# A decoder layer's MLP with seven half-size products in place of eight, its rows passed through DRAM

## The reference

```
h = x + rms_norm(m, n_mix_post)
f = square(relu(rms_norm(h, n_ffn_pre) @ w_up)) @ w_down
return h + rms_norm(f, n_ffn_post), new_buf, S_new
```

## Time and profile before

| | |
|---|---|
| runs | 1697.92, 1699.09, 1698.83 us, median 1698.83 |
| profiled execution, span | 1695.9 us (its own time is one of those above, 2 to 3 us more than its span) |
| TensorE matmuls busy | 1634.7 us, 96% of the span, 10272 matmuls recorded |
| VectorE, ScalarE, GpSimd busy | 749.9, 320.5, 678.8 us |
| granted clock of TensorE, mean | 0.989 of full |
| DMA | 101.18 MB, 60 GB/s over the span |

### The profile page before, as it was taken

One profiled execution on the slowest core, in us unless ns is written; L12 is line 12 of the kernel. 1 busy time (PEld: TensorE's weight loads), 2 busy tenths in 40 slices (PEclk: granted clock), 3 DMA queues, 4 the chain that ended last, 5 costly groups with the idle time before them and its releaser, 6 DMA issues.

```text
span 1695.9 us, 26474 instructions
## 1 busy us (share of the span) xinstructions
PE 1634.7 (96%) x10272; PEld 1609.6 (95%) x10272; DVE 749.9 (44%) x907; ACT 320.5 (19%) x407; POOL 678.8 (40%) x548
## 2 busy tenths in 40 slices
PE   5999999999999998999998999999999999999994
PEld 4999999899999997999998999999999999999993
DVE  5898969354482334101515623232232323222338
ACT  4100000422311223000214311011111111110122
POOL 3334444232254223434474334343444434343444
PEclk9999999999999999999999999999999999999997
DMA  4211121123221331111321011111111111111112
GB/s 167 88 50 44 49 57 46 30 76 99 75 94 50 95 105 32 43 49 43 145 75 31 26 51 44 49 43 49 44 45 48 44 49 43 49 43 49 44 26 100
DMA packets 57771, 101.18 MB, mean 60 GB/s; under 512 B 6128, under 2 KB 21232, under 8 KB 57344
## 3 DMA queue, kind: packets, MB, share of 16 engines
q1 hardware_dynamic: 43792, 76.97, 15.6%
q10 hardware_dynamic: 13936, 23.60, 4.2%
HBM read 91.00 MB, written 9.55 MB: 59 GB/s over the span
## 4 chain that ended last, share of the span: by engine, by line
PE 94%; DVE 4%; DMA 1%; issue 1%; ACT 1%; ACTq 0%; SPq 0%; DVEq 0%
PE ps L465 84%; PE ps L723 3%; DVE mix L1549 1%; PE ps L813 1%; PE ps L646 1%; PE ps L565 1%; DVE xn_l L1216 1%; PE ps L564 1%; PE ps L491 1%; PE ps L568 1%; PE ps L579 1%; DMA x_in<-xT_dram 1%; PE ps L549 0%; PE ps L554 0%; DVE x_in L1212 0%
## 5 line engine op out<-in xcount | busy, mean ns | idle before, releaser
L368 POOL TENSOR_TENSOR w_h<-raw,zero 128x512 fp32r<-128x512 f32 x250 | 268.7, 1075 | 928.4 <-PE ps L465 806.4
L371 POOL TENSOR_TENSOR w_l<-raw,w_h 128x512 fp32r<-128x512 f32 x250 | 332.3, 1329 | 19.6
L1504 DVE TENSOR_TENSOR mix<-ps,mix 128x1032 f32<-128x1032 f32 x120 | 147.9, 1233 | 300.6 <-PE ps L465 300.6
L465 PE MATMUL ps<-xn_h,w_h 128*128 128x344 f32 x1128 | 248.2, 326 | 5.0 <-DVE xn_l L1216 4.0
L465 PE MATMUL ps<-xn_l,w_h 128*128 128x344 f32 x1128 | 241.9, 320 | 0.0
L465 PE MATMUL ps<-xn_h,w_l 128*128 128x344 f32 x1128 | 241.0, 320 | 0.0
L465 PEld LDWEIGHTS ps<-xn_h,w_h 128*128 128x128 f32 x1128 | 190.2, 188 | 9.4 <-issue 4.8
L465 PEld LDWEIGHTS ps<-xn_l,w_h 128*128 128x128 f32 x1128 | 191.2, 189 | 0.1
L465 PEld LDWEIGHTS ps<-xn_h,w_l 128*128 128x128 f32 x1128 | 188.8, 188 | 0.0
L465 PE MATMUL ps<-fx_h,w_h 128*128 128x344 f32 x768 | 169.7, 322 | 5.8 <-ACT fx_h L1099 5.4
L465 PE MATMUL ps<-fx_l,w_h 128*128 128x344 f32 x768 | 168.8, 321 | 0.0
(11 more groups left out here) (201 smaller groups left out, 1934.3 us busy)
## 6 DMA issues: line engine op xcount, KB each, us to landing
raw<-wseq_dram SPq DMA_DIRECT2D x264, 256.0 KB, 2.6
rope<-rope_dram ACTq DMA_DIRECT2D x2, 2064.0 KB, 8.1
h_res<-xT_dram ACTq DMA_DIRECT2D x1, 4128.0 KB, 12.8
s_dec<-s_in_dram ACTq DMA_DIRECT2D x16, 256.0 KB, 2.8
v_bc<-v_sample_scratch ACTq DMA_DIRECT2D x16, 256.0 KB, 3.8
rets_dram<-s_dec ACTq DMA_DIRECT2D x16, 256.0 KB, 2.2
x_in<-xT_dram SPq DMA_DIRECT2D x2, 1376.0 KB, 12.9
yT_dram<-h_res SPq DMA_DIRECT2D x3, 860.0 KB, 3.9
```

Source lines behind the costliest of these rows:

```text
L368: pool.tensor_tensor(hi, raw[:, s, :], zero[:, 0:1].broadcast_to([P, SLOT]), ALU.add).then_inc(w_hi, 1)
L371: pool.tensor_tensor(lo, raw[:, s, :], hi.bitcast(F32), ALU.subtract).then_inc(w_split, 1)
L465: out = pe.matmul(pch(g, c), w[a][:, place_, sub * P:(sub + 1) * P], xs[b][:, k, c * CH:(c + 1) * CH], start=(first and n == 0), stop=(las ...
L1504: dve.tensor_tensor(t3(mix[:, m, :]), pset(g), t3(mix[:, m, :]), ALU.add).then_inc(ps_free[g % 2], 1)
```

## The change

The two matrix products of the MLP are each done with Strassen's scheme (in the Winograd form) one level deep: the weights and the rows are cut in halves of channels (4 tiles of 8) and halves of tokens (2 x 516), and seven products of half-size operands replace eight, with sums of quadrants ahead of and behind them.

- Tokens are now cut into halves of 516 and matmuls of 258 tokens (`HT`, `HC`).
- A unit is a pair of output tiles: seven products of 4 k-tiles x 3 parts x 2 matmuls, 168 matmuls of 258 columns. The first two units of up (`DIRECT`) stay as before, in 344-column matmuls; then there are 14 units of up and 16 of down (`NV` = 30).
- All of up comes first. The hidden rows of each unit are kept as 7 operands, summed on VectorE (`hidden_sums`, 4 sums of 128x516), stored by the SP queue to `uscr` in DRAM (`store_unit`, 264 + 528 + 1056 KB) and loaded back for down, one group of 4 units at a time (`load_operand`, 28 loads of 1032 KB). `h` goes to DRAM and comes back as well (`hscr`), since the down result `fac` takes its place.
- The operands of down are split again: high part on ScalarE (`staged_hi`, 128x4x516), low part on VectorE (`staged_lo`, two of 128x2x516).
- Weight sums are made on VectorE (`first_sums`, `last_sum`, 4 of 128x512 a unit). The high part of a weight slot is now copied by ScalarE (`high`), GpSimd makes the low part alone (`low`), 7 a unit, in a ring of three.
- PSUM is used as three pairs of banks that rotate (`BANKS`); ScalarE and VectorE take the products out (`up_unit`, `down_unit`).
- The final norm goes by two halves of tokens, both after nearly all of down, with fac and h for 516 tokens at a time.

The core of the diff:

```diff
+HT = T // 2
+HC = HT // 2
+QK = KT // 2
+RING = 3
+DIRECT = 2
+UNITS = FFN // P // 2
+UPV = UNITS - DIRECT
+NV = UPV + UNITS
+STEPS = 7
...
+            def store_unit(u):
+                g, j = divmod(u, QK)
+                sp.wait_ge(t_u, 4 * u + 4)
+                sp.dma_start(uscr[g, 0, :, j, :], hq_row(u, 0)).then_inc(st_u[u % 2], 16)
...
+            def product(v, i, between=None):
+                q = STEPS * v + i
+                a, b, c = BANKS[v]
+                n = (a, b, c, a, c, a, a)[i]
+                x, kh, th = X_OF[i]
+                pe.wait_ge(q_lo, q + 1)
...
+                for s in range(2):
+                    if s == 0 or i == 6:
+                        bank_ready(v, i, s)
+                    for kk in range(QK):
+                        for m, (wa, xb) in enumerate(PARTS):
+                            at_ = th * HT + s * HC
+                            out = pe.matmul(ps[:, 2 * n + s, 0:HC], RINGS[q % RING][wa][:, kk * P:(kk + 1) * P],
+                                            OPS[x][xb][:, QK * kh + kk, at_:at_ + HC],
...
+            def low(v, i):
+                q = STEPS * v + i
+                src = (raw[:, 0, :], raw[:, 1, :], sum_y[:], raw[:, 2, :], raw[:, 3, :], sum_x[:], sum_y[:])[i]
+                hi, lo = RINGS[q % RING]
+                pool.wait_ge(q_hi, q + 1)
+                pool.tensor_tensor(lo, src, hi.bitcast(F32), ALU.subtract).then_inc(q_lo, 1)
...
+            def high(v, i):
+                q = STEPS * v + i
+                if q < RING:
+                    act.wait_ge(mm, E_FFN + 1 + q)
+                else:
+                    act.wait_ge(pm, 2 * (q - RING) + 2)
...
+                act.activation(RINGS[q % RING][0], src, ACT.Copy).then_inc(q_hi, 1)
...
+            high(0, 0)
+            high(0, 1)
+            stored(act, 0)
+            direct_out(1, 0, E_FFN + 2)
+            direct_out(1, 1, E_FFN + 4)
+            high(0, 2)
...
+            def first_sums(v):
+                if v:
+                    dve.wait_ge(q_lo, STEPS * v)
+                else:
+                    dve.wait_ge(mm, E_FFN + 4)
...
+            def down_unit(v):
...
+                evicted(dve, v, "e4")
+                add(m2, 0, c, step_done(v, 4))
+                if p == 3 and g + 1 < GROUPS:
+                    staged_lo(STEPS * (g + 1) + 2)
+                evicted(dve, v, "e3")
+                for s in range(2):
+                    dve.wait_ge(pm, step_done(v, 5) - 1 + s)
+                    f = two(fac[:, m2, HALVES[1]])[:, s, :]
+                    dve.tensor_tensor(f, ps[:, 2 * a + s, 0:HC], f, ALU.add).then_inc(ev_d, 1)
...
+            for v in range(UPV):
+                if v == 0:
+                    first_sums(0)
+                    hidden_sums(0)
+                up_unit(v)
+            for v in range(UPV, NV):
+                down_unit(v)
+            root_argument(0, 3)
+            out_norm(0, 3)
+            root_argument(1, BANKS[NV - 1][1])
             out_residual(0)
+            out_norm(1, BANKS[NV - 1][1])
             out_residual(1)
```

More of the change, by code:

```diff
@@ L340, in _ @@
                                  ).then_inc(raw_ld[s], 16)
[L341 to L348, removed]
+            sp.wait_ge(h_dve, CHUNKS)
+            sp.wait_ge(h_pool, CHUNKS)
@@ L731, in _, with up_mms @@
             FX = (fx_h, fx_l)
-            HID = (hid_h, hid_l)
+            def up_mms(c, g, k, slot, first, last):
+                for n, (a, b) in enumerate(PARTS):
+                    out = pe.matmul(pch(g, c), DIRECT_W[slot][a][:, (k % SLOT_TILES) * P:(k % SLOT_TILES + 1) * P],
+                                    FX[b][:, k, c * CH:(c + 1) * CH],
+                                    start=(first and n == 0), stop=(last and n == 2))
+                return out
             for c, j in ((0, 0), (1, 0), (0, 1), (1, 1), (2, 0), (2, 1)):
@@ L748, in _ @@
                     mix_stat(2)
[L750 to L758, removed]
-                        out = tile_mms((slot + m // 2) % HL, FB * (m % 2) + k, HID, FB * (b % 2) + k,
-                                       g + m, k == 0, k == FB - 1)
-                    out.then_inc(mm, 1)
@@ L819, in _ @@
-            out_stat(CHUNKS - 1)
+            for j in range(2):
+                g = G_FFN + 2 + j
+                free_set(pe, g)
+                for half in range(2):
+                    pe.wait_ge(w_split, S_FFN + 4 + 2 * j + half + 1)
+                    for k in range(QK * half, QK * half + QK):
+                        for c in range(CHUNKS):
+                            out = up_mms(c, g, k, 2 * j + half, k == 0, k == KT - 1)
+                    out.then_inc(mm, 1)
+            OPS = ((fx_h, fx_l), (tx_h, tx_l))
@@ new lines, in h_stat, with f_ones @@
+            def h_stat(t):
+                if t == 0:
+                    pe.wait_ge(hs_ad, 2 * KT)
+                else:
+                    pe.wait_ge(h_cp, 1)
+                for s in range(2):
+                    out = pe.matmul(ps[:, 6 + s, 0:HC], ones[:], hms[:, t * HT + s * HC:t * HT + (s + 1) * HC],
+                                    start=True, stop=True)
+                out.then_inc(h_st, 1)
+            def f_ones(row, first, last, n):
+                for s in range(2):
+                    out = pe.matmul(ps[:, 2 * n + s, 0:HC], ones[:], hq_g[:, row, s * HC:(s + 1) * HC],
+                                    start=first, stop=last)
+                return out
@@ new lines, in f_stat_first @@
+            def f_stat_first():
+                pe.wait_ge(f_ad, 6)
+                pe.wait_ge(h_cp, 2)
+                f_ones(0, True, True, 3).then_inc(f_st, 1)
+            for v in range(NV):
+                for i in range(STEPS):
+                    product(v, i, f_stat_first if (v, i) == (NV - 1, STEPS - 1) else None)
+                    if v == 3 and i in (0, 3):
+                        h_stat(i // 3)
+            pe.wait_ge(f_ad, 8)
+            evicted(pe, NV - 1, "e2")
+            f_ones(4, True, False, BANKS[NV - 1][1])
```

812 lines of the change are left out of this document (563 added, 249 removed).

## The result

The changed kernel takes **1687.03 us** (four runs, 1685.12 to 1688.15) beside 1698.38 for the kernel before on the same chip: ratio 0.9938, 95% interval 0.9925 to 0.9951, 11.4 us faster. The forecast was 1658.1, 40.7 us faster. The direction holds and the time lies inside the range, but nearly three quarters of the forecast gain are missing. One execution of an experiment (`e11_gpsimd`) took 3955.7 us, for no reason that is known, and is left out of its numbers.

What follows compares the result with a forecast made beforehand. The MLP was taken as bound by matmul count and start-to-start time, its end by the norm. 977.4 + 13.5 + 1.6 + 615.4 + 1.8 + 16 + 29.5 = 1655.2 us span; median 2.9 above, 1658.1; range 1606 to 1702.

Steps and rivals of the forecast that it cites:

- The price: Time per 258-column matmul at full clock: 122.1 ns taken, 5040 of them 615.4 us; case of 118 to 125 ns, 60%.
- shared supply: Rival on the matmul time: weight load and stream share one supply, 129.1 ns at 258 columns, 1693 us; 15%.
- load that takes 157.9 ns: Rival: the weight load under a stream sets the pace at 157.9 ns whatever the width, 180 us more, 1838; 9%.
- the floor: Rival: the weight load alone sets the lowest time of a matmul, 112 ns, giving 1607 us; 8%.
- The plain unit: In a plain up unit, ScalarE, VectorE, GpSimd and DMA work fits under 20.5 us of matmuls, costed at nothing.
- the ring rival: Rival: the ring of three weight slots waits in every unit, 2.5 us each, 75 us more, 1733; 8%.
- The handover: Between direct units and first product, TensorE idles while unit 0's data is made and stored and relu follows: 13.5 us.
- The seams: Three joins of down groups at 3.3 us each, 10, and up to down, 6: together 16 us, bounds 0 and 40.
- The statistics: 8 f32 statistics matmuls of 258 columns among the fast units, 217 ns each: 1.8 us.
- The direct units: First two units of up in 344-column matmuls at 157.9 ns, ending at 977.4 us.
- The tail: After the last product: last taking, final norm to +24 us, then 1290 KB out in 5.1; 29.5 us.

Runs made afterwards that it cites:

- e11_gpsimd: Changed kernel with GpSimd's low parts of the weights in units 17 and 18 cut to 8 of 512 columns: 1679.28 us, ratio 0.9903.
- e10_first: Changed kernel with unit 0's hidden rows summed before first weight sums and four low parts, copy of h issued behind first fast unit's store: 1669.58 us, 0.9843.
- e12_all: Changed kernel with the edits to joins, first unit, statistics and up-to-down loads together, last up unit's rows made and stored a unit later: 1642.32 us, 0.9684.
- e3_stat: Changed kernel with the column sums of h and their two roots moved from the fourth fast unit to the fifth: 1683.60 us, 0.9918.

## Why the prediction was right and wrong

- **The price.** Right in kind, too dear. 122.1 was chosen over 118.4; measured 119.8, between the two: of the surplus over 2.4 GHz, 3.7 ns go with the matmul by the line above and the rest with the columns. It gave back 11.6 us. The rivals on the price are settled: no shared supply (it gives 129.1 ns at 258 columns, and by its formula 214 at 512 where 232.0 were measured), no load that takes 157.9 ns; the floor exists, but at 258 columns the stream is just above it.
- **The plain unit** costed at nothing: right. Units 4 to 12 have no idle time in 181 us, so the ring rival is false.
- **The handover**, 13.5 against 13.0: right by its size, for a reason that was half wrong. I had the data made in 5.2 us and the store land 6.7 us later, on a free queue. They took 4.6 and 7.2, so two errors cancel (the profile counts the store as 1806 KB, not 1848). The sum left out the copy of h issued ahead of the store, so it gave no hint that making the data earlier would not help.
- **"The seams. [...] Together 16; bounds 0 and 40"** is the step that failed: 47.1 us were measured, 17.9 from up to down and 29.2 at the three joins, outside the bounds. It is the whole of what is missing: the span is 30.3 us over the forecast, and the seams are 31.1 over it. I compared a single third low part with one product (4.7 against 2.93), as if VectorE were on time when it began; the two before it had already used the slack, and VectorE began the taking ahead of it 1.8 us after TensorE had finished the product. In the next unit I summed the operations that exclude each other (21.9 against 20.5) but set VectorE's takings, 4.9 us, at nothing; the unit takes 24.0. I counted neither the half clock behind each break nor, from up to down, that ScalarE's taking stands behind the operand it waits for.
- **The statistics**, 1.8: only the matmuls were costed, as 8 of 217 ns, where the trace has 8 in unit 3 and 4 in unit 29: each f32 matmul of the program stands there as two (the 24 in the earlier trace rows are 12 in the program). The last addition ends 4.9 us into unit 3, 1.9 after the product behind which TensorE wants it; that wait and its tail made it 7.4.
- **The direct units**, 4.7 us late: GpSimd's splits, 1.33 us in the earlier trace rows, take 2.6 to 3.2 us beside VectorE's operations of 2064 elements, which I had not put beside them. TensorE waits for one of them, and the granted clock is 0.50 from 957.7 to 961.1 behind it. This rests on the trace alone; in e10_first and e12_all the wait is 2.5 and 2.6 us.

```profile
957.08 0.40 PE L881 MATMUL ps<-fx_h,w_h 128*128 128x344 f32 x1 [2.42 <-POOL w_l L524]
```

- **The tail**, 29.5 against 30.4: right by its size. The terms given add up to 29.1 (24 and 5.1), and the 2.4 ns an element of GpSimd are 2.5 in the earlier trace rows; measured are 22.8 to the end of VectorE's work and 7.7 for the output, so here too errors cancel.

The price was costed from rows of the same operation and came out within 2%. What was missed is, in most cases, work on two engines or queues that was costed alone and met there.

## What to carry to other kernels

Where a stage ends, list all that the helping engine owes in that stretch, the takings included, at the duration it has when its neighbour runs too, and compare it product by product with the matmuls, not unit by unit. A break of 2 to 4 us in TensorE here cost 1.5 to 2.5 us more behind it, in matmuls at half clock. When moving an operation earlier changes nothing, look at what stands ahead of it on the next queue.

## What the runs showed of the hardware

- fp32r matmuls: 0.446 ns a column and 3.7 ns from 344 to 512 columns; 111.6 ns at 220, 180 and 128 alike.
- In the unit of 64 columns the granted clock fell to 0.50 though TensorE did not stand idle; in the unit of 128 before it the clock stayed at 1.00.
- VectorE's pair of low parts: 2.37 us alone, 2.9 to 3.9 beside GpSimd. GpSimd's low part of 512 elements: 1.3 us alone, up to 2.3 beside VectorE's operations of 1032 elements and 3.2 beside those of 2064.
- A plain f32 matmul of the program is two in the trace: 8 for 4 in e3_stat, 217 ns each at 258 columns.
- The last part (1032 KB) of a store of three parts landed in 5.9 us, and in 11.3 with 4128 KB issued 5.6 us ahead of it on the same queue.
